# First mixer: the triangular inverse in stages of four blocks (Horner form), transposes for products, four masks for seven

## The chip, the cores and the metric

One Trainium2 chip, of which the kernel uses one core. The metric is the device time of one execution in microseconds; the time of a kernel is the median of its runs.

## The reference, cut to what matters

The program is three transformer layers in float32 over 512 tokens of width 1024. The change touches only the first mixer, a chunked gated delta rule with 8 heads of 128 columns. For each head it solves a unit lower triangular system:

```python
a_low = jnp.where(strict, jnp.einsum('bhncd,bhnsd->bhncs', k_beta, k) * decay, 0.0)
eye = jnp.eye(CHUNK, dtype=q.dtype)
rhs = jnp.concatenate([v * beta[..., None], k_beta * jnp.exp(g_cum)[..., None]], axis=-1)
sol = lax.linalg.triangular_solve(eye + a_low, rhs, left_side=True, lower=True,
                                  unit_diagonal=True)
u, w = sol[..., :dv], sol[..., dv:]
```

Around it stand the dense projection of the layer input (`proj = hn @ w_in`), a causal convolution of width 4, the norms of q and k, and the scan over chunks that uses `u` and `w`. The kernel works with chunks of 128 tokens instead of 64, so each head has four chunks (`TT = 4`) and for each a 128x128 triangle to invert.

## The kernel before, in words

Each engine has its own instruction stream, written out by hand, and the streams meet only at semaphores: the order of the lines is the order of the work.

The first mixer is a loop over eight heads, `period(p)` on every engine. On TensorE a period has 32 slots. In slot `i` stands first one dense block of the projection for head p+1 (`dense_for`: three fp32r matmuls of 128x128 by 128x512 for the high and low halves, L1716 to L1718), then what `rest_of(p-1, i)` has in that slot (the scan over chunks of the head before: w at slot 0, L1955; `vn`, L1963 and L1965; outputs and state, L1970 to L1977; the sum of squares of the output, L1981), then `front(p, i)` (rows of decays, L1894 and L1895; products of keys and queries, L1899 and L1902; transposes of k and v, L1907 and L1912; transposes of the masked matrix, L1917) and `level(p, i)`, the inverse. At slot 23 stand besides the sums of squares of the next head's q and k (`qk_sums`, L1883 and L1884). In head 0 the slots of `front` and `level` are moved by the table `FIRST_HEAD` and the sums stand at slot 24. The last head has no dense blocks of a next head; 15 blocks of the output projection stand in its even slots from 2 on (`OUT_AT`).

The inverse before goes through seven levels of blocks (1, 2, 4, ... 64). `TI` holds the inverse so far, `T` its transpose, four 128x128 matrices each. Level 0 is one minus the masked matrix (`AM`, made on GpSimd, L1615) and, through a transpose on TensorE (L1917), the same for `T`. Each of the six other levels has two steps:

- the X step (slots `X_AT`, L1930): `AM` times `T`, four fp32 matmuls of 128x128 into bank 5, which ScalarE copies to `X` (L520, `inverse_x`);
- the Y step (slots `Y_AT`): four products of `X` and `TI` into bank 6 (L1941), which VectorE subtracts from `T` (L1169), and four into bank 7 (L1944), which VectorE subtracts from `TI` (L1173). The last level has no L1941.

Four such matmuls, one for each chunk, are called a group below. The profiler records two rows of TensorE for each fp32 matmul of this kind and one for each transpose, so a group of matmuls is x8 and a group of transposes x4.

ScalarE has in a period, in this order from slot 19 on: `inverse_x(p, 3)`, the two steps of the output norm (`out_rstd`, L536 and L538), half of the split of weights (`hi_half`, L512), a load of a function table and Silu and Square of the next head's q and k (`evac_qk`, L483 and L485), and `inverse_x(p, 4)`. TensorE's `qk_sums` at slot 23 waits for the Square (semaphore `qk_sq`). Then `qk_rstds` (L491 to L494) follows. VectorE does the convolutions (L1072, L1075), the low halves of the weights (`lo_half`, L1148), the state of the scan (L1159, L1162) and the subtractions of the inverse. A dense block at slot 0 waits for VectorE's convolution of v (`conv_v`), the one at slot 16 for that of q (`conv_q`).

Of the kernel before, what the change touches and what calls it, by code (L numbers as in the profile page):

```python
# [13 lines left out]
F32 = mybir.dt.float32  # L14
F32R = mybir.dt.float32r
# [5 lines left out]
P = 128  # L21
# [11 lines left out]
LEVELS = 7  # L33
# [14 lines left out]
MATS = ("ident", "ones", "rot", "prefix", "suffix", "future", "cap", "lvl0", "lvl1", "lvl2", "lvl3", "lvl4", "lvl5", "lvl6")  # L48
# [27 lines left out]
X_AT, Y_AT = (7, 11, 15, 19, 23, 27), (9, 13, 17, 21, 25, 29)  # L76
W_AT, VN_AT, OS_AT, OSS_AT = 0, (1, 5, 9, 13), (3, 7, 11, 15), 19
FIRST_HEAD = {0: 5, 1: 6, 3: 8, 5: 10, 7: 12, 9: 13, 11: 15, 13: 16, 15: 18, 17: 20, 19: 21, 21: 23, 23: 25, 25: 26, 27: 28, 29: 30}
# [38 lines left out]
def build(nc, io):  # L117
    with ExitStack() as ctx:
# [30 lines left out]
        with ExitStack() as gdn:  # L149
# [20 lines left out]
            rows_r = sb("rows_r", [48, SEQ], F32R, gdn)  # L170
            sel = sb("sel", [48, 2, 2, P], F32R, gdn)
            ba_wh = sb("ba_wh", [P, P], F32R, gdn)
            ba_wl = sb("ba_wl", [P, P], F32R, gdn)
# [26 lines left out]
        with ExitStack() as mix:  # L200
# [24 lines left out]
            cosT, sinS = trig("prefix"), trig("lvl0")  # L225
# [61 lines left out]
        part_done = sem("part_done")  # L287
# [52 lines left out]
        def _(act):  # L340
# [103 lines left out]
            act.activation(ba_wh[:, :], ba_w, ACT.Copy)  # L444
# [108 lines left out]
            def period(p):  # L553
# [14 lines left out]
                hi_half(2 * p + 3, 0)  # L568
                if p:
                    values_out(g, 1, 2)  # L570
# [5 lines left out]
                inverse_x(p, 0)  # L576
                if p:
                    values_out(g, 2, 2)
                if last:
                    out_fill(3)  # L580
                inverse_x(p, 1)
                if p:
                    values_out(g, 3, 2)
                if last:
                    out_fill(4)
                inverse_x(p, 2)
                if p:
                    out_squares(g, 3)
                if dense:
                    hi_half(2 * p + 4, 0)  # L590
                if last:
                    out_fill(5)
                inverse_x(p, 3)
# [317 lines left out]
        def _(dve):  # L911
# [130 lines left out]
            dve.tensor_tensor(ba_wl[:, :], ba_w, ba_wh[:, :].bitcast(F32), ALU.subtract)  # L1042
# [121 lines left out]
            def inverse_y(h, n):  # L1164

                if n < 5:
                    dve.wait_ge(y_done, 11 * h + 2 * n + 1)
                    dve.wait_ge(t_made, 6 * h + n + 1)
                    dve.tensor_tensor(T[:, :, :], T[:, :, :], bank(6), ALU.subtract).then_inc(t_made, 1)  # L1169
                ti = TI[:, h % 2, :, :]  # L1170
                dve.wait_ge(y_done, 11 * h + (2 * n + 2 if n < 5 else 11))
                dve.wait_ge(ti_made, 7 * h + n + 1)
# [11 lines left out]
            def period(p):  # L1184
# [25 lines left out]
                one = mat("ident").unsqueeze(1).to_broadcast([P, TT, P])  # L1210
                dve.wait_ge(am_made, 7 * p + 1)
                dve.tensor_tensor(TI[:, r, :, :], one, AM[:, 0, :, :], ALU.subtract).then_inc(ti_made, 1)
                dve.wait_ge(amt_done, p + 1)
                dve.tensor_tensor(T[:, :, :], one, bank(4), ALU.subtract).then_inc(t_made, 1)
                if last:
                    out_low(2)
                if p:
                    state(g, 1, 2)
                lo_half(2 * p + 3, 0)
                inverse_y(p, 0)  # L1220
# [7 lines left out]
                inverse_y(p, 1)  # L1228
# [4 lines left out]
                inverse_y(p, 2)  # L1233
# [4 lines left out]
                inverse_y(p, 3)  # L1238
                if p:
                    scale_out(g, 3)  # L1240
                if dense:
                    lo_half(2 * p + 4, 0)
# [1330 lines left out]
```

## Time and profile before

| what | value |
|---|---|
| median of 3 runs | 2312.74 us (2311.11 to 2314.26) |
| profiled execution, its own time | 2316.1 us |
| its span | 2314.3 us |
| TensorE busy | 2238.7 us, 97% of the span |
| VectorE, ScalarE, GpSimd busy | 1130.4, 918.5, 323.6 us |
| TensorE's share of the chain that ended last | 90% |
| granted clock of TensorE, mean | 0.990 of 2.4 GHz |

The profiled execution is one of a kind with the others: it took 3.4 us more than the median. Busy shares are means over stages; the first mixer's eight periods lie between about 69 and 462 us of the span. In rows of the timeline, neighbouring rows of TensorE overlap, since each row holds the whole way of its columns through the array: what one group costs there is the distance from its start to the next start.

### The profile page before, as it was taken

The numbers are of one execution on the slowest core, as the hardware profiler recorded it, in microseconds if no ns is written. First come the engines' busy times: TensorE is split into PE (matmuls) and PEld (weight loads), VectorE is DVE, ScalarE is ACT, GpSimd is POOL, SyncE is SP. The second block draws the span as 40 slices with busy tenths as digits, with TensorE's granted clock in tenths as the row PEclk, the third lists the DMA queues.
The fourth block names the chain that finished last, engine by engine and source line by source line (L and its number), as shares of the span: only waits on it lengthen the run. The fifth ranks groups of instructions, "written<-read, shape, count | busy, mean of one in ns | idle before, by whom it ended". The sixth has DMA issues, their size and how long they took to land.

```text
span 2314.3 us, 28733 instructions
## 1 busy us (share of the span) xinstructions
PE 2238.7 (97%) x11172; PEld 1840.8 (80%) x11172; DVE 1130.4 (49%) x1437; ACT 918.5 (40%) x1235; POOL 323.6 (14%) x271
## 2 busy tenths in 40 slices
PE   7899999999999999998999999999999999999998
PEld 4688888778888887976788888887788787888886
DVE  4556556544444323355444442254665655655522
ACT  4444444433223225466322321244665554444311
POOL 0123222230000110001300001100100025222211
PEclk9899999999999999999999999999999999999999
DMA  3311110112222222210222222231211213222221
GB/s 135 92 55 37 41 51 37 37 73 91 101 98 91 94 106 73 92 55 19 73 96 104 91 94 106 91 133 69 69 55 69 69 37 127 97 103 91 93 108 55
DMA packets 30607, 185.61 MB, mean 80 GB/s; under 512 B 3104, under 2 KB 5536, under 8 KB 10160
## 3 DMA queue, kind: packets, MB, share of 16 engines
q1 hardware_dynamic: 28496, 176.66, 21.4%
q0 software_dynamic: 2016, 7.60, 1.0%
q8 instruction: 69, 1.13, 0.2%
q14 instruction: 26, 0.21, 0.0%
HBM read 180.02 MB, written 7.37 MB: 81 GB/s over the span
## 4 chain that ended last, share of the span: by engine, by line
PE 90%; ACT 4%; DVE 4%; issue 1%; DMA 0%; SPq 0%; POOL 0%; DVEq 0%; ACTq 0%; POOLq 0%
PE ps L1716 25%; PE ps L1718 24%; PE ps L1717 24%; PE ps L1930 1%; PE ps L1944 1%; PE ps L1941 1%; PE ps L2375 1%; PE ps L2318 1%; PE ps L2358 1%; PE ps L2155 1%; DVE convd L1075 1%; PE ps L2385 1%; PE ps L2193 1%; DVE wl L920 1%; ACT wh L349 0%
## 5 line engine op out<-in xcount | busy, mean ns | idle before, releaser
L1716 PE MATMUL ps<-xh,wh 128*128 128x512 f32 x1888 | 767.2, 406 | 30.4 <-DVE wl L920 17.1
L1718 PE MATMUL ps<-xh,wl 128*128 128x512 f32 x1888 | 740.6, 392 | 0.0
L1717 PE MATMUL ps<-xl,wh 128*128 128x512 f32 x1888 | 740.1, 392 | 0.0
L349 ACT ACTIVATE wh<-raw 128x2048 fp32r<-128x2048 f32 x144 | 275.3, 1914 | 545.0 <-PE ps L1718 544.7
L920 DVE TENSOR_TENSOR wl<-raw,wh 128x2048 fp32r<-128x2048 f32 x144 | 336.7, 2338 | 310.9 <-ACT wh L349 310.9
L1716 PEld LDWEIGHTS ps<-xh,wh 128*128 128x128 f32 x1888 | 357.8, 189 | 115.3 <-issue 26.5
L1718 PEld LDWEIGHTS ps<-xh,wl 128*128 128x128 f32 x1888 | 357.0, 189 | 76.9
L1717 PEld LDWEIGHTS ps<-xl,wh 128*128 128x128 f32 x1888 | 357.8, 190 | 71.9 <-issue 4.5
L1716 PE MATMUL ps<-hid_h,wh 128*128 128x512 f32 x528 | 208.0, 394 | 0.0
L1718 PE MATMUL ps<-hid_h,wl 128*128 128x512 f32 x528 | 207.0, 392 | 0.0
L1717 PE MATMUL ps<-hid_l,wh 128*128 128x512 f32 x528 | 204.9, 388 | 0.0
L998 DVE TENSOR_TENSOR scaled<-ps,rstd 128x1024 f32<-128x1024 f32 x44 | 53.9, 1225 | 192.9 <-PE ps L1718 192.9
L1615 POOL TENSOR_TENSOR AM<-AT,mats 128x512 f32<-128x512 f32 x56 | 76.3, 1369 | 332.2 <-DVE AT L1196 196.9
L1718 PEld LDWEIGHTS ps<-hid_h,wl 128*128 128x128 f32 x528 | 99.1, 188 | 23.2
L1717 PEld LDWEIGHTS ps<-hid_l,wh 128*128 128x128 f32 x528 | 99.1, 188 | 22.2
L1716 PEld LDWEIGHTS ps<-hid_h,wh 128*128 128x128 f32 x528 | 99.3, 188 | 19.7
L1581 POOL TENSOR_TENSOR sq<-hT 128x512 f32<-128x512 f32 x41 | 48.3, 1178 | 292.6 <-DVE hT L1032 257.6
L520 ACT ACTIVATE X<-ps 128x512 f32<-128x512 f32 x48 | 28.7, 597 | 146.9 <-PE ps L1930 146.9
L1576 POOL TENSOR_TENSOR ssq<-hT 128x512 f32<-128x512 f32 x6 | 6.2, 1041 | 563.0 <-DVE hT L1032 507.0
L1169 DVE TENSOR_TENSOR T<-T,ps 128x512 f32<-128x512 f32 x40 | 27.6, 689 | 104.6 <-PE ps L1941 104.4
L422 ACT ACTIVATE hid_h<-gu 128x512 f32 (+1 forms) x44 | 27.8, 632 | 110.2 <-DVE gu L1008 110.2
L998 DVE TENSOR_TENSOR gu<-ps,rstd 128x1024 f32<-128x1024 f32 x22 | 26.9, 1224 | 85.8 <-PE ps L1718 85.8
(343 smaller groups left out, 2938.7 us busy)
## 6 DMA issues: line engine op xcount, KB each, us to landing
raw<-in_stream SPq DMA_DIRECT2D x159, 1024.0 KB, 4.8
hankd<-tabd SPq DMA_DIRECT2D x1, 3072.0 KB, 16.9
hank<-hankd POOLq DMA_DIRECT2D x4, 768.0 KB, 5.0
hT<-in_xT SPq DMA_DIRECT2D x4, 512.0 KB, 6.0
keepd<-hT POOLq DMA_DIRECT2D x1, 2048.0 KB, 11.3
hT<-keepd POOLq DMA_DIRECT2D x8, 256.0 KB, 4.4
out<-hT SPq DMA_DIRECT2D x8, 256.0 KB, 2.1
raw<-in_stream SPq DMA_DIRECT2D x2, 512.0 KB, 9.0
```

The lines of the kernel that those rows point to most:

```text
L349: act.activation(wh[:, s, :], raw[:, s, :], ACT.Copy).then_inc(hi_made, 1)
L422: act.activation(hid_h[:, 2 * it + j, :], prod, ACT.Copy).then_inc(hid_hi_made, 1)
L520: act.activation(X[:, :, :], blocks4(5), ACT.Copy).then_inc(x_made, 1)
L920: dve.tensor_tensor(wl[:, s, :], raw[:, s, :], wh[:, s, :].bitcast(F32), ALU.subtract).then_inc(lo_made, 1)
L998: dve.tensor_tensor(to[:, :, :], ps[:, b:b + 2, :], rstd[:, :].unsqueeze(1).to_broadcast([P, 2, SEQ]), ALU.mult).then_inc(gu_made, 1)
L1075: dve.scalar_tensor_tensor(convd[:, i, d:SEQ], ps[:, b, 0:SEQ - d], w, convd[:, i, d:SEQ], ALU.mult, ALU.add).then_inc(conv_step, 1)
L1169: dve.tensor_tensor(T[:, :, :], T[:, :, :], bank(6), ALU.subtract).then_inc(t_made, 1)
L1581: pool.tensor_tensor(sq[:, :], hT[:, c, :], hT[:, c, :], ALU.mult).then_inc(squared, 1)
L1615: pool.tensor_tensor(AM[:, l % 2, :, :], AT[:, :, :], m, ALU.mult).then_inc(am_made, 1)
L1716: pe.matmul(out, w_hi, a_hi, start=start, stop=False)
L1717: pe.matmul(out, w_hi, a_lo, start=False, stop=False)
L1718: return pe.matmul(out, w_lo, a_hi, start=False, stop=stop)
```

## The change

The seven levels become four stages with blocks of 1, 4, 16 and 64 (`STAGES`), and the masks are `below1`, `below4`, `below16`, `below64`; the masks of 4 and 16 are transposed. A stage with four blocks inverts two levels at once: with M the strictly block-triangular part times the inverse of the diagonal blocks, M to the fourth power is zero and the inverse is a sum of three powers, taken in Horner form.

- Stage 0: `U` = one minus the transposed A (VectorE), then "square" and "cube" on TensorE, each `AM` times `U`, and after each one minus the product on VectorE, which gives `T`. "turn0" transposes `T` on TensorE and ScalarE copies it to `TI`.
- Stages 1 and 2: "scale" (`AM` times `TI`, a group), ScalarE's copy with sign to `X` (`inverse_x`), "first", "second", "third" (groups with `X`, after each VectorE adds `T`), and "turn" (transposes `T`), with ScalarE's copy to `TI` (`turned`).
- Last stage, two blocks: "x" and "y", as the last level before.
- A second group of transposes (of `AT`, unmasked) joins the one at slot 5, and ScalarE copies it to `DT` (`make_a`), from which GpSimd makes the two transposed masks.

The slots of the inverse, and with them those of `vn`, outputs and the sum of squares, are set anew:

```diff
-X_AT, Y_AT = (7, 11, 15, 19, 23, 27), (9, 13, 17, 21, 25, 29)
-W_AT, VN_AT, OS_AT, OSS_AT = 0, (1, 5, 9, 13), (3, 7, 11, 15), 19
+INVERSE_AT = {"square": 7, "cube": 9, "turn0": 10, "scale1": 12, "first1": 13, "second1": 15, "third1": 17, "turn1": 18,
+              "scale2": 20, "first2": 21, "second2": 23, "third2": 25, "turn2": 26, "x": 28, "y": 30}
+W_AT, VN_AT, OS_AT, OSS_AT = 0, (1, 5, 9, 15), (3, 7, 12, 17), 20
...
+            def make_a(h):
+                act.wait_ge(amt_done, h + 1)
+                act.activation(DT[:, :, :], blocks4(5), ACT.Copy).then_inc(a_made, 1)
+
+            def turned(h, n):
+                act.wait_ge(turned_done, 3 * h + n + 1)
+                act.activation(TI[:, h % 2, :, :], blocks4((4, 4, 6)[n]), ACT.Copy).then_inc(ti_made, 1)
+
             def inverse_x(h, n):
-                act.wait_ge(x_done, 6 * h + n + 1)
-                act.activation(X[:, :, :], blocks4(5), ACT.Copy).then_inc(x_made, 1)
+                act.wait_ge(x_done, 3 * h + n + 1)
+                act.activation(X[:, :, :], blocks4(5), ACT.Copy, scale=1.0 if n == 2 else -1.0).then_inc(x_made, 1)
...
                 hi_half(2 * p + 3, 0)
+                make_a(p)
                 if p:
                     values_out(g, 1, 2)
                 hi_half(2 * p + 3, 1)
...
-                inverse_x(p, 3)
+                inverse_x(p, 1)
                 if p:
                     out_rstd(g, 2)
                 if dense:
                     hi_half(2 * p + 4, 1)
                     evac_qk(p + 1)
-                inverse_x(p, 4)
-                if dense:
                     qk_rstds(p + 1)
-                inverse_x(p, 5)
+                turned(p, 2)
+                inverse_x(p, 2)
...
+            def inverse_t(h, n):
+
+                bank_of = (4, 6, 7, 6, 7, 6, 7, 6, 7)
+                dve.wait_ge(*((amt_done, h + 1) if n == 0 else (y_done, 9 * h + n)))
+                if n:
+                    dve.wait_ge(t_made, 9 * h + n)
+                if n < 3:
+                    one = mat("ident").unsqueeze(1).to_broadcast([P, TT, P])
+                    dve.tensor_tensor((T if n == 2 else U)[:, :, :], one, bank(bank_of[n]), ALU.subtract).then_inc(t_made, 1)
+                else:
+                    dve.tensor_tensor((T if n % 3 == 2 else U)[:, :, :], T[:, :, :], bank(bank_of[n]), ALU.add).then_inc(t_made, 1)
...
                 elif slot == AMT_AT:
-                    pe.wait_ge(am_made, 7 * p + 1)
+                    pe.wait_ge(am_made, 4 * p + 1)
+                    pe.wait_ge(attn_made, p + 1)
                     for c in range(TT):
                         m = pe.transpose(ps[:, 4, cs(c)], AM[:, 0, c, :], mat("ident"))
+                    for c in range(TT):
+                        m = pe.transpose(ps[:, 5, cs(c)], AT[:, c, :], mat("ident"))
                     m.then_inc(amt_done, 1)
...
+                    elif name[:4] == "turn":
+                        pe.wait_ge(t_made, 9 * p + 3 * k + 3)
                         for c in range(TT):
+                            m = pe.transpose(ps[:, (4, 4, 6)[k], cs(c)], T[:, c, :], mat("ident"))
+                        m.then_inc(turned_done, 1)
+                    elif name[:5] == "scale":
+                        pe.wait_ge(ti_made, 4 * p + k)
+                        pe.wait_ge(am_made, 4 * p + k + 1)
+                        if k == 1:
+                            pe.wait_ge(a_made, p + 1)
+                        each(5, AM[:, k % 2, :, :], ti).then_inc(x_done, 1)
+                    elif name[:5] == "first":
+                        pe.wait_ge(x_made, 3 * p + k)
+                        each(5 + k, X, T).then_inc(y_done, 1)
+                    elif name[:6] == "second":
+                        pe.wait_ge(t_made, 9 * p + 3 * k + 1)
+                        each(8 - k, X, U).then_inc(y_done, 1)
+                    elif name[:5] == "third":
+                        pe.wait_ge(t_made, 9 * p + 3 * k + 2)
+                        each(5 + k, X, U).then_inc(y_done, 1)
```

How the order changes on TensorE, in a middle head, from the sum of squares of the output (L1981) to the sums for q and k (L1883, L1884). Before, with slots 19 to 23; the groups x4 are the inverse:

```order
L1981 MATMUL ps<-on,mats 128x512
L1930 MATMUL ps<-T,AM 128x128 x4
L1716 MATMUL ps<-xh,wh 128x512
L1717 MATMUL ps<-xl,wh 128x512
L1718 MATMUL ps<-xh,wl 128x512
...
L1941 MATMUL ps<-X,TI 128x128 x4
L1944 MATMUL ps<-TI,X 128x128 x4
...
L1930 MATMUL ps<-T,AM 128x128 x4
L1883 MATMUL ps<-sqk,mats 128x512
L1884 MATMUL ps<-sqk,mats 128x512
```

The first "..." is one more dense block (slot 21), the second is two (slots 22 and 23). Of the change, slots 20 to 23, where "..." is the two dense blocks of slots 22 and 23 (L1941 is here "scale2", "first2" and "second2" in turn, L2021 the sum of squares, L1900 and L1901 the sums for q and k):

```order
L2021 MATMUL ps<-on,mats 128x512
L1941 MATMUL ps<-TI,AM 128x128 x4
L1733 MATMUL ps<-xh,wh 128x512
L1734 MATMUL ps<-xl,wh 128x512
L1735 MATMUL ps<-xh,wl 128x512
L1941 MATMUL ps<-T,X 128x128 x4
...
L1941 MATMUL ps<-U,X 128x128 x4
L1900 MATMUL ps<-sqk,mats 128x512
L1901 MATMUL ps<-sqk,mats 128x512
```

Between the group that ScalarE's `inverse_x` waits for and the sums stood four dense blocks and three groups; now three dense blocks and two groups stand there.

On ScalarE, the same place before (from L520, `inverse_x(p, 3)`, to the reciprocal roots of q and k, L494, and the last `inverse_x`):

```order
L520 ACTIVATE X<-ps 128x512
L536 ACTIVATE on<-ps,vec 128x512
L538 ACTIVATE on<-on 128x512
L512 ACTIVATE wh<-raw 128x1024
L483 ACT_TABLE_LOAD
L483 ACTIVATE qkvz<-convd 128x1024
L485 ACTIVATE sqk<-qkvz 128x1024
L520 ACTIVATE X<-ps 128x512
L353 ACT_TABLE_LOAD
L491 ACTIVATE sqk<-ps,vec 128x512
L492 ACTIVATE sqk<-ps,vec 128x512
L494 ACTIVATE sqk<-sqk 128x1024
```

And of the change (L530 is `inverse_x`, L526 `turned`):

```order
L530 ACTIVATE X<-ps 128x512
L546 ACTIVATE on<-ps,vec 128x512
L548 ACTIVATE on<-on 128x512
L514 ACTIVATE wh<-raw 128x1024
L485 ACT_TABLE_LOAD
L485 ACTIVATE qkvz<-convd 128x1024
L487 ACTIVATE sqk<-qkvz 128x1024
L355 ACT_TABLE_LOAD
L493 ACTIVATE sqk<-ps,vec 128x512
L494 ACTIVATE sqk<-ps,vec 128x512
L496 ACTIVATE sqk<-sqk 128x1024
L526 ACTIVATE TI<-ps 128x512
```

From the copy of `X` to the Square nothing is moved; the copy of `X` behind the Square is gone and `turned` stands behind the roots.

On TensorE, slots 9 to 12 of the change, where "cube" and "turn0" (L1962) follow each other with one dense block between, and "scale1" comes after the outputs of the scan:

```order
L1941 MATMUL ps<-U,AM 128x128 x4
L1733 MATMUL ps<-xh,wh 128x512
L1734 MATMUL ps<-xl,wh 128x512
L1735 MATMUL ps<-xh,wl 128x512
L1962 MATMUL ps<-mats,T 128x128 x4
...
L2010 MATMUL ps<-qd,S 128x128
L2015 MATMUL ps<-attnT,vn 128x128
L2017 MATMUL ps<-vn,kd 128x128
L1941 MATMUL ps<-TI,AM 128x128 x4
```

Before, in a middle head, every two neighbouring groups of the inverse that wait for each other had two dense blocks between them; now "cube" and "turn0", "scale1" and "first1", "third1" and "turn1", "scale2" and "first2", "third2" and "turn2" have one.

## Rows read from the trace of the kernel before

**Rows 1.** The page: busy time and instructions of each engine

```profile
PE 2238.7 (97%) x11172; PEld 1840.8 (80%) x11172; DVE 1130.4 (49%) x1437; ACT 918.5 (40%) x1235; POOL 323.6 (14%) x271
```

**Rows 2.** Windows, heads 1 to 6: busy us by engine, granted clock, DMA

```profile
118.49:419.29 300.80, 293.76 (x1859) 254.44 (x1857) 178.93 (x270) 138.29 (x199) 77.02 (x54) 1.00 0.12 42
```

**Rows 3.** Timeline of TensorE, head 3: start, us, instruction, idle before it

```profile
225.09 0.60 PE L1907 MATMUL ps<-mats,qkvz 128*128 128x128 f32 x4
225.53 0.60 PE L1912 MATMUL ps<-mats,qkvz 128*128 128x128 f32 x4
...
227.79 0.60 PE L1917 MATMUL ps<-mats,AM 128*128 128x128 f32 x4
...
249.50 1.05 PE L1930 MATMUL ps<-T,AM 128*128 128x128 f32 x8
...
251.78 1.05 PE L1941 MATMUL ps<-X,TI 128*128 128x128 f32 x8
252.67 1.06 PE L1944 MATMUL ps<-TI,X 128*128 128x128 f32 x8
253.49 0.47 PE L1716 MATMUL ps<-xh,wh 128*128 128x512 f32 x1
...
254.26 0.40 PE L1716 MATMUL ps<-xh,wh 128*128 128x512 f32 x1
...
254.95 1.05 PE L1930 MATMUL ps<-T,AM 128*128 128x128 f32 x8
256.89 1.12 PE L1883 MATMUL ps<-sqk,mats 128*128 128x512 f32 x2 [0.88 <-ACT sqk L485]
```

**Rows 4.** Timeline of VectorE, head 3

```profile
228.43 0.69 DVE L1214 TENSOR_TENSOR T<-mats,ps 128x512 f32<-128x512 f32 x1 [0.16 <-PE ps L1917]
...
252.87 0.69 DVE L1169 TENSOR_TENSOR T<-T,ps 128x512 f32<-128x512 f32 x1 [1.73 <-PE ps L1941]
```

**Rows 5.** Timeline of ScalarE, head 3

```profile
250.59 0.60 ACT L520 ACTIVATE X<-ps 128x512 f32<-128x512 f32 x1 [4.15 <-PE ps L1930]
...
255.78 1.06 ACT L485 ACTIVATE sqk<-qkvz 128x1024 f32<-128x1024 f32 x1
```

**Rows 6.** Timeline of TensorE, the start of head 4

```profile
268.17 0.50 PE L1716 MATMUL ps<-xh,wh 128*128 128x512 f32 x1 [0.19 <-DVE convd L1075]
...
268.98 1.05 PE L1955 MATMUL ps<-TI,kbe 128*128 128x128 f32 x8
```

**Rows 7.** Timeline of TensorE, last head

```profile
419.29 1.16 PE L1955 MATMUL ps<-TI,kbe 128*128 128x128 f32 x8 [0.78 <-DVE TI L1173]
...
457.81 1.05 PE L1930 MATMUL ps<-T,AM 128*128 128x128 f32 x8
...
459.55 1.16 PE L1944 MATMUL ps<-TI,X 128*128 128x128 f32 x8
...
461.48 1.16 PE L1955 MATMUL ps<-TI,kbe 128*128 128x128 f32 x8
```

**Rows 8.** Timeline of TensorE, head 0 and the start of head 1

```profile
87.78 0.50 PE L1716 MATMUL ps<-xh,wh 128*128 128x512 f32 x1 [2.65 <-DVE convd L1075]
...
88.58 1.70 PE L1941 MATMUL ps<-X,TI 128*128 128x128 f32 x8
...
91.64 0.74 PE L1716 MATMUL ps<-xh,wh 128*128 128x512 f32 x1
...
104.28 1.13 PE L1883 MATMUL ps<-sqk,mats 128*128 128x512 f32 x2 [1.24 <-ACT sqk L485]
...
117.69 0.50 PE L1716 MATMUL ps<-xh,wh 128*128 128x512 f32 x1 [1.84 <-DVE convd L1075]
...
118.49 1.05 PE L1955 MATMUL ps<-TI,kbe 128*128 128x128 f32 x8
```

**Rows 9.** Windows behind two idle times of TensorE: columns as in rows 2

```profile
88.60:91.90 3.30, 3.30 (x18) 3.30 (x17) 0.69 (x1) 0.00 (x0) 0.00 (x0) 0.53 0.13 52
119.30:122.60 3.30, 3.30 (x24) 2.69 (x23) 1.67 (x5) 1.99 (x4) 0.00 (x0) 1.00 0.00 0
```

More of the change, by code:

```diff
@@ L32 @@
 NEG = -1e30
-LEVELS = 7
+STAGES = (1, 4, 16, 64)
 LN_EXP_SET = 6
@@ L1209, in period @@
                     out_low(1)
[L1210 to L1214, printed above, removed]
+                inverse_t(p, 0)
                 if last:
@@ L1602, in period @@
                 g, r = p - 1, p % 2
-                for l in range(LEVELS):
-                    if l == 0:
+                for n, size in enumerate(STAGES):
+                    if n == 0:
                         pool.wait_ge(at_made, p + 1)
-                    elif l == 2:
+                    elif n == 1:
                         pool.wait_ge(eg_made, p + 1)
@@ L1914, in front, with each @@
                 elif slot == AMT_AT:
-                    pe.wait_ge(am_made, 7 * p + 1)
+                    pe.wait_ge(am_made, 4 * p + 1)
+                    pe.wait_ge(attn_made, p + 1)
                     for c in range(TT):
                         m = pe.transpose(ps[:, 4, cs(c)], AM[:, 0, c, :], mat("ident"))
+                    for c in range(TT):
+                        m = pe.transpose(ps[:, 5, cs(c)], AT[:, c, :], mat("ident"))
                     m.then_inc(amt_done, 1)
+            def each(b, left, right):
+                for c in range(TT):
+                    m = pe.matmul(ps[:, b, cs(c)], left[:, c, :], right[:, c, :], start=True, stop=True)
+                return m
@@ L1937, in level @@
                         pe.wait_ge(kdkbe_made, p + 1)
+                        each(6, AM[:, 0, :, :], U).then_inc(y_done, 1)
+                    elif name == "cube":
+                        pe.wait_ge(t_made, 9 * p + 2)
                         pe.wait_ge(vb_made, p + 1)
[L1939 removed]
+                        each(7, AM[:, 0, :, :], U).then_inc(y_done, 1)
+                    elif name[:4] == "turn":
+                        pe.wait_ge(t_made, 9 * p + 3 * k + 3)
                         for c in range(TT):
[L1941 to L1942 removed]
@@ L1943, in level @@
-                    for c in range(TT):
-                        m = pe.matmul(ps[:, 7, cs(c)], X[:, c, :], ti[:, c, :], start=True, stop=True)
-                    m.then_inc(y_done, 1)
+                            m = pe.transpose(ps[:, (4, 4, 6)[k], cs(c)], T[:, c, :], mat("ident"))
[15 more added lines that the diff above has]
+                        each(5 + k, X, U).then_inc(y_done, 1)
+                    elif name == "x":
+                        pe.wait_ge(ti_made, 4 * p + 3)
+                        pe.wait_ge(am_made, 4 * p + 4)
+                        each(5, AM[:, 1, :, :], T).then_inc(x_done, 1)
+                    else:
+                        pe.wait_ge(x_made, 3 * p + 3)
+                        each(7, X, ti).then_inc(y_done, 1)
```

106 lines of the change are left out of this document (47 added, 59 removed).

## The prediction

> **What bounds the kernel now.** I read the page first: TensorE is busy for 2238.7 us [rows 1]. In heads 1 to 6 of the first mixer it is busy for 293.76 of 300.80 us [rows 2], so a head takes 300.80 / 6 = 50.13 us and hardly more than its TensorE work. Next I read the timeline of one middle head, TensorE first, and looked at every idle time with its releaser. There are two in a head. One is 0.88 us ahead of the sums for q and k, released by ScalarE's Square [rows 3]; the other is 0.19 us at slot 0, released by the convolution of v [rows 6]. Measured from the time at which TensorE could have gone on, they cost more: the X group starts at 254.95 and takes 0.89, so the sums could have started at 255.84 and did at 256.89, 1.05 us later. At slot 0 the like comes to about 0.45 us. So in a middle head 50.13 = 48.6 of work + 1.5 of waiting. Then the two ends: head 0, which waits longer (2.65, 1.24, 1.84 us) [rows 8], and the last head, which has few dense blocks to cover its chain.
>
> **Prices.** From start to next start a group of four fp32 matmuls takes 252.67 - 251.78 = 0.89 us. A group of four transposes takes 225.53 - 225.09 = 0.44. Of two dense blocks behind a group the first takes 0.77 and the second 0.69 [rows 3]; the group ahead of them then counts 0.82, so I take 0.89 and 0.70 throughout and nothing for the switch. From the start of a group to the engine that reads its bank: 252.87 - 251.78 = 1.09 us; 0.64 for transposes [rows 3, 4]. ScalarE then takes 0.60, VectorE 0.69 [rows 4, 5], and TensorE goes on about 0.05 later (Square's end 256.84, sums 256.89 [rows 3, 5]). A chain group, block, group takes 1.59 us without a wait. Through ScalarE it took 459.55 - 457.81 = 1.74 [rows 7], and the group behind such a wait takes some 0.10 more. I price a link through ScalarE with one block as cover at 0.25 us, one through VectorE, 0.09 slower, at 0.35.
>
> **What goes and comes on TensorE.** A head had 17 groups of matmuls and one of transposes in its inverse. Now it has 12 and 5: square, cube, two times (scale, first, second, third), x, y; and two at slot 5, three turns. That is 5 x 0.89 - 4 x 0.44 = 2.69 us less work in a head, 21.5 us in eight, if nothing waits. Work in a middle head falls from 48.6 to 45.9.
>
> A rule speaks to the size of this. The Trainium skill, page "TensorE: Matmul & The Clock Gate", section "Terms", calls the transpose mode four times faster for FP32. By that a group of transposes would be 0.22 us and a head would save 5 x 0.89 - 4 x 0.22 = 3.57, so 0.9 more; eight heads would give 2308 instead of my 2315.5 if none of it were lost to waits. The rows show half the price of a matmul group, not a quarter, and I stay with them.
>
> **What waits instead, middle head.** Five links now have one block as cover. Cube to turn0, third1 to turn1 and third2 to turn2 go through VectorE: 3 x 0.35. Scale1 to first1 and scale2 to first2 go through ScalarE: 2 x 0.25. Together 1.55 us. The others have two blocks, or a block and work of the scan, and I find them covered: square to cube has 1.4 of blocks and 0.44 of `vn` against 0.69 of VectorE; second1 to third1 the same. VectorE's 1.22 us of `lo_half` lies between square and cube and ends 0.8 us before cube does. GpSimd's masks are each asked for 4 us or more after their input is there. The convolution of q ends 0.3 us before slot 16 asks for it, that of v 0.2 us before slot 0; a delay there would cost itself. The 0.45 at slot 0 goes.
>
> The large one is ahead of the sums. ScalarE goes from the copy of `X` through `out_rstd`, `hi_half`, a table load, Silu and Square without a stop: 250.59 to 256.84, 6.25 us [rows 5], and this series is not changed. So the sums start 1.09 + 6.25 + 0.05 = 7.39 us after the start of the group that this copy waits for. Before, that group was X at slot 19 (249.50), and TensorE had 6.34 us of work until the sums. Now it is scale2 at slot 20, with scale2 itself, three blocks, first2 with its wait of 0.25, and second2 behind it: 3 x 0.89 + 3 x 0.70 + 0.25 = 5.0. The wait is 7.39 - 5.0 = 2.4 us in place of 1.05. In idle time as the timeline counts it, about 2.25.
>
> Sum for a middle head: 45.9 + 1.55 + 2.4 = 49.85 against 50.13, so -0.3 us, and -1.8 for six. A second way gives -0.45: scale2 starts 0.2 us later in its head than X did (one block more, two groups and a bit less), and behind the sums there are two groups and a wait less in work: -0.65 + 0.2. I keep the first.
>
> **Head 0.** I walked it by the same prices. Before, the convolution of q, which VectorE starts only after two subtractions, held slot 16 to 87.78 [rows 8]. Now it comes at 87.4, but three groups that stood ahead of the sums for q and k no longer do: TensorE has scale2 at 95.9, ScalarE's series (without `out_rstd`, 5.1 us from the copy's start) ends at 102.5, and the sums start there instead of at 104.28. The wait ahead of them is 2.7 us idle instead of 1.24. Behind them TensorE needs 12.6 us until head 1, which starts at 115.1 instead of 118.49: -3.4 us. The walk has an error of 1 to 1.5 us.
>
> **The last head.** It has 15 blocks as cover and no sums. Its chain is longer now: 12 links of 1.8 and three turns of 1.3 against 12 of 1.8. ScalarE's `make_a`, ahead of `values_out` and the fill of the third chunk, delays VectorE's `out_low` and with it square to cube by some 1.2 us, first1 and first2 have no block in their slots (0.85 each), and y now stands in the last slot but one with nothing behind it. Walked from the transposes at slot 5, the last w group starts at 462.7 against 461.48 [rows 7]: +1.2 us.
>
> **The clock.** In head 0 idle time of 2.65 us was followed by a granted clock of 0.53, which is 1.2 GHz, while 1.84 us was followed by 1.00 [rows 8, 9]. Two groups that take 1.71 then took 91.64 - 88.58 = 3.06, and the block behind them 0.25 more: 1.6 us for one fall. The new waits lie between these rows: 2.25 in six heads, 2.7 in head 0. Nothing in the trace of before says whether 2.25 does it. Bounds are none of the seven and all seven; I count head 0's and 3.5 of the other six, 4.5 falls. Part of a fall may lie in the wait itself, so 1.5 us each: +6.8. The fall that head 0 had before, behind 2.65 us, is on the side of before in the 3.4; its wait of now (2.2 idle) could fall as well, which is in the range.
>
> **Sum.** -1.8 - 3.4 + 1.2 = -4.0 without the clock, +2.8 with it. The profiled execution took 2316.1, so 2318.9 for its like; it lies 3.4 us above the median, and the difference is what carries over: 2312.7 + 2.8 = 2315.5.
>
> **Rivals.** Within 0.2% is within 4.6 us, about what a measurement of this kernel can tell from no change.
>
> (a) The forecast: the wait ahead of the sums grows, the clock falls behind some of the seven. 2311 to 2319. Chance 0.45.
>
> (b) The wait grows, and the clock falls behind none or one: 2312.7 - 4.0 = 2308.7, up to 2310. For it: the clock held at 1.84 us. Against: it fell at 2.65. Chance 0.2.
>
> (c) The clock falls in every head, twice in head 0: eight falls are +12, 2312.7 - 4.0 + 12 = 2320.7; this is the slower side. It decides from 2.25 us of idle time being enough. For it: six heads are alike, so what one does the others may do. Against: the wait need not lie the same way each time, and the fall adds to the head's length. Chance 0.22. The Trainium skill, same page, section "Part 4: PE-mode transpose", says that a transpose does not count as busy TensorE for the clock; with 28 transposes in a head where 12 were, that speaks for this case. The transposes at slot 3 in the old trace ran at full clock, but nothing there puts them beside a long wait.
>
> (d) The sums don't wait longer, because ScalarE gets through earlier than I read, and only the five short links cost: 45.9 + 1.55 = 47.45 in a head, -2.7 x 6 - 3.4 + 1.2 = -18.4, 2294. Against it stands that this series on ScalarE is the same instruction for instruction. Chance 0.07.
>
> (e) A delay on VectorE in each head: the convolution of q or v comes late, with margins of 0.2 to 0.3 us. A GpSimd mask beside `lo_half` could add 0.75. On top of the forecast that is +4, 2319. Chance 0.06.
>
> **How the numbers follow.** Likeliest is (a), 2315.5. The range from 2306 to 2322 takes in (a), (b), (c) and (e) with an error of 2 us of the walks, and leaves out (d) and the far ends. Faster by over 0.2% (under 2308.1): (d) and half of (b), 0.18. Slower (over 2317.3): (c), half of (e), and the upper part of (a), 0.32. The rest is 0.50.
>
> **What would show it.** In the new trace: 12 groups of inverse matmuls and 5 of its transposes in a head instead of 17 and 1; the sums for q and k wait for Square with about 2.2 us in heads 1 to 6; short waits of 0.1 to 0.3 for VectorE at the turns; w groups 49.8 us apart where the clock holds and 51.3 where it falls; granted clock 0.5 behind some of the waits; about 43.4 us from the last head's first w group to the next. It is wrong if the wait ahead of the sums is under 1.5 us, or if a releaser that I called covered (convolution, mask, `lo_half`) heads the list of waits.

## The result and the profile after

The changed kernel takes 2316.18 us (median of 22 runs, 2314.18 to 2319.83) against 2312.68 (22 runs, 2310.82 to 2315.56): a ratio of 1.0015, interval 1.0008 to 1.0021. It is 3.5 us slower, a difference that the interval tells from zero, and lies within 0.2% of before. Its profiled execution took 2318.6 us with a span of 2316.5, at a mean granted clock of 0.987 against 0.990 before.

The first rows of the page, busy time of each engine:

```profile
PE 2231.8 (96%) x10980; PEld 1817.9 (78%) x10980; DVE 1117.2 (48%) x1413; ACT 924.4 (40%) x1243; POOL 283.5 (12%) x247
```

TensorE is busy for 6.9 us less than before [rows 1], GpSimd for 40, and still the kernel is not faster. The timeline of TensorE in a middle head, from the scale group of stage 2 to the first w group, columns: start, duration, engine, line, operation, operands, shapes and count, and in brackets idle time and its releaser:

```profile
191.45 0.66 PE L1962 MATMUL ps<-mats,T 128*128 128x128 f32 x4
...
194.19 1.05 PE L1941 MATMUL ps<-TI,AM 128*128 128x128 f32 x8
...
195.94 1.16 PE L1941 MATMUL ps<-T,X 128*128 128x128 f32 x8
...
198.32 1.05 PE L1941 MATMUL ps<-U,X 128*128 128x128 f32 x8
201.59 1.12 PE L1900 MATMUL ps<-sqk,mats 128*128 128x512 f32 x2 [2.21 <-ACT sqk L487]
202.55 1.85 PE L1901 MATMUL ps<-sqk,mats 128*128 128x512 f32 x2
203.41 1.42 PE L1733 MATMUL ps<-xh,wh 128*128 128x512 f32 x1
204.62 0.63 PE L1734 MATMUL ps<-xl,wh 128*128 128x512 f32 x1
205.05 0.63 PE L1735 MATMUL ps<-xh,wl 128*128 128x512 f32 x1
...
206.42 1.05 PE L1941 MATMUL ps<-U,X 128*128 128x128 f32 x8
...
208.26 0.66 PE L1962 MATMUL ps<-mats,T 128*128 128x128 f32 x4
```

L1941 is now every group of the inverse, L1962 a turn, L1900 and L1901 the sums for q and k, L1733 to L1735 a dense block. The sums wait 2.21 us for Square where it was 0.88 [rows 3]. From the start of scale2 to the sums it is 201.59 - 194.19 = 7.40 us, and ScalarE's series in that time:

```profile
195.28 0.60 ACT L530 ACTIVATE X<-ps 128x512 f32<-128x512 f32 x1 [2.54 <-PE ps L1941]
195.78 0.68 ACT L546 ACTIVATE on<-ps,vec 128x512 f32<-128x512 f32 x1
196.49 0.63 ACT L548 ACTIVATE on<-on 128x512 f32<-128x512 f32 x1
197.03 1.05 ACT L514 ACTIVATE wh<-raw 128x1024 fp32r<-128x1024 f32 x1
198.09 1.28 ACT L485 ACT_TABLE_LOAD   x1
199.39 1.06 ACT L485 ACTIVATE qkvz<-convd 128x1024 f32<-128x1024 f32 x1
200.48 1.06 ACT L487 ACTIVATE sqk<-qkvz 128x1024 f32<-128x1024 f32 x1
```

It has no gap, and takes 201.54 - 195.28 = 6.26 us, as it did [rows 5]. In the TensorE rows behind the sums a dense row lasts 0.63 where it otherwise lasts 0.39 to 0.40: the clock. The view by windows, columns us, then TensorE, its weight loads, VectorE, ScalarE and GpSimd, then granted clock, DMA share and GB/s; first the wait and the sums, then what follows; next two stretches of head 1, whose sums start at 151.82 behind a wait of the same length; last the stretch behind the start of the sums of head 6, at 407.22:

```profile
199.19:202.60 3.41, 1.20 (x5) 0.54 (x4) 1.49 (x3) 3.35 (x4) 1.27 (x1) 1.00 0.00 0
202.70:206.00 3.30, 3.30 (x8) 1.89 (x7) 0.00 (x0) 1.67 (x4) 0.00 (x0) 0.50 0.00 0
151.50:154.80 3.30, 2.98 (x10) 1.81 (x10) 0.00 (x0) 2.51 (x4) 0.83 (x1) 1.00 0.00 0
154.90:158.20 3.30, 3.22 (x21) 2.56 (x20) 2.08 (x4) 1.86 (x3) 0.00 (x0) 1.00 0.00 0
407.50:410.80 3.30, 3.30 (x5) 1.22 (x5) 0.00 (x0) 0.97 (x1) 0.23 (x1) 0.50 0.00 0
```

In this head the clock falls to 0.50, 1.2 GHz, about 1 us after TensorE goes on, and stays there for about 3.4 us. About half of that is lost: by the lengths of the heads below, 1.6 us. In the heads that follow the fall begins earlier, and in head 6 it takes in nearly all of the sums. And the stretches from one first w group to the next, of TensorE alone: head 1, head 2, head 6 and the last.

```profile
113.55:163.30 49.75, 47.29 (x288) 1.00 0.13 45
163.30:214.69 51.39, 48.94 (x287) 0.97 0.11 42
368.94:419.94 51.00, 48.46 (x285) 0.97 0.11 39
419.94:463.20 43.26, 37.37 (x231) 0.96 0.09 31
```

A head whose clock holds takes 49.75 us against 50.13; one in which it falls 51.39 to 51.43 (heads 3 to 5 are as head 2). Head 1 alone held, heads 2 to 6 fell. In head 0 it fell twice:

```profile
82.68 0.50 PE L1733 MATMUL ps<-xh,wh 128*128 128x512 f32 x1 [2.22 <-DVE convd L1084]
...
99.46 1.38 PE L1900 MATMUL ps<-sqk,mats 128*128 128x512 f32 x2 [2.54 <-ACT sqk L487]
```

**Where the mixer's time went in these two traces.** From the rows of decays of head 0 to its first w group it is 48.54 us against 48.69 (65.01 to 113.55, and 69.80 to 118.49): -0.15. Heads 1 to 6 take 306.39 us against 300.80 [rows 2]: +5.6. The last head takes 43.26 against 42.19 [rows 7]: +1.07. Together +6.5. The profiled executions differ by 2.5 us only, since the one of before comes to head 0 4.8 us later (69.80 against 65.01), though both programs do the same work on TensorE up to there. Most of that, 3.6 us, comes about between 11 and 28 us, with a granted clock of 0.57 from 20 to 24 us where the one of after had 1.00 (windows of TensorE alone, before and then after):

```profile
20.00:24.00 4.00, 2.52 (x7) 0.57 0.00 0
20.00:24.00 4.00, 3.89 (x18) 1.00 0.13 20
```

Such falls outside the mixer come and go from one execution to the next: in the nine traces of the changed kernel and its variants below, which are the same program up to there, head 0 starts between 64.53 and 68.61 us. So the medians, 3.5 apart, are the measure of the change, and one trace against another is read by stretches only.

### The profile page after: what moved, and what is told of

The parts are those of the page before. It is cut to its first block, busy times and chain, and to the rows that moved or that the text cites. A ratio compares the mean times of both kernels' runs of the same rounds, so it can differ in the third digit from the quotient of the medians.

```text
span 2316.5 us, 28229 instructions
## 1 busy us (share of the span) xinstructions
PE 2231.8 (96%) x10980; PEld 1817.9 (78%) x10980; DVE 1117.2 (48%) x1413; ACT 924.4 (40%) x1243; POOL 283.5 (12%) x247
## 4 chain that ended last, share of the span: by engine, by line
PE 91%; ACT 4%; DVE 4%; issue 1%; DMA 0%; POOL 0%; SPq 0%; DVEq 0%; ACTq 0%; POOLq 0%
PE ps L1733 25%; PE ps L1735 24%; PE ps L1734 24%; PE ps L1941 3%; PE ps L2415 1%; PE ps L2358 1%; PE ps L2398 1%; PE ps L2195 1%; PE ps L2425 1%; PE ps L2233 1%; PE ps L1962 1%; DVE wl L929 1%; PE ps L1901 1%; PE ps L1900 0%; DVE T L1183 0%
## 5 line engine op out<-in xcount | busy, mean ns | idle before, releaser
L1733 PE MATMUL ps<-xh,wh 128*128 128x512 f32 x1888 | 772.1, 409 | 25.8 <-DVE wl L929 17.1
L1735 PE MATMUL ps<-xh,wl 128*128 128x512 f32 x1888 | 741.1, 393 | 0.0
L1733 PEld LDWEIGHTS ps<-xh,wh 128*128 128x128 f32 x1888 | 358.8, 190 | 109.0 <-issue 26.0
L1735 PEld LDWEIGHTS ps<-xh,wl 128*128 128x128 f32 x1888 | 357.4, 189 | 76.8
L1733 PE MATMUL ps<-hid_h,wh 128*128 128x512 f32 x528 | 208.0, 394 | 0.0
L1735 PE MATMUL ps<-hid_h,wl 128*128 128x512 f32 x528 | 207.0, 392 | 0.0
L1735 PEld LDWEIGHTS ps<-hid_h,wl 128*128 128x128 f32 x528 | 99.1, 188 | 23.2
L1733 PEld LDWEIGHTS ps<-hid_h,wh 128*128 128x128 f32 x528 | 99.3, 188 | 19.7
L1599 POOL TENSOR_TENSOR ssq<-ssq,sq 128x512 f32<-128x512 f32 x41 | 61.4, 1497 | 3.2
L827 ACT ACTIVATE prob<-ps,nmax 128x512 f32<-128x512 f32 x32 | 22.0, 689 | 89.4 <-DVE nmax L1484 89.2
L1084 DVE SCALAR_TENSOR_TENSOR convd<-ps,vec,convd 128x511 f32<-128x511 f32 (+2 forms) x72 | 53.8, 748 | 2.3
```

Of the source, the lines that this page charges most:

```text
L1084: dve.scalar_tensor_tensor(convd[:, i, d:SEQ], ps[:, b, 0:SEQ - d], w, convd[:, i, d:SEQ], ALU.mult, ALU.add).then_inc(conv_step, 1)
L1599: pool.tensor_tensor(ssq[:, :], ssq[:, :], sq[:, :], ALU.add).then_inc(summed, 1)
L1733: pe.matmul(out, w_hi, a_hi, start=start, stop=False)
L1735: return pe.matmul(out, w_lo, a_hi, start=False, stop=stop)
```

## The experiments

Kernels are compared with runs of the kernel before on the same chip: medians 2313.49 us for the first four, 2313.83 for the next four and 2313.01 for the last two. "A head" is the distance between first w groups of two middle heads in the trace.

**Theory.** The Horner form itself gains about 5 us, and the falls of the clock behind the longer wait ahead of the sums take more than that. Rivals: the length of the wait costs, not the clock; or transposes let the clock fall.

### Filling the wait: matmuls, transposes

Work that nobody reads goes into the idle time, so that TensorE is busy while the sums still start when Square is done. It adds work and takes none away. With matmuls:

```diff
+                if n:
+                    for _ in range(9):
+                        pe.matmul(ps[:, 4, :], wh[:, 1, 0:P], xh[:, 0, :], start=True, stop=True)
                 pe.wait_ge(qk_sq, n + 1)
```

> The changed kernel with nine extra fp32r matmuls (0.23 us each, 2.1 us in all, into bank 4, which the sums overwrite) ahead of the wait for Square in each of the seven heads that have the sums. They fit into the wait of 2.2 us idle, so nothing else moves. Theory (the falls of the clock behind this wait cost 1.6 us each): no granted clock of 0.5 behind the sums in any head, the middle heads all 49.75 us apart, and 5 to 6 falls fewer: 8 to 10 us less than the changed kernel, about 2307. Rival (the longer wait and the longer chain are the loss, and the clock is a symptom that other waits hide): within 1 us of the changed kernel, 2316.

And with transposes in their place:

```diff
+                if n:
+                    for k in range(20):
+                        pe.transpose(ps[:, 4, (k % 4) * P:(k % 4 + 1) * P], T[:, k % 4, :], mat("ident"))
                 pe.wait_ge(qk_sq, n + 1)
```

> As fill_mm, with twenty transposes of 128x128 (0.11 us each, 2.2 us in all) in place of the nine matmuls. If transposes keep the clock up as matmuls do: the same 2307. If a transpose does not count as busy TensorE for the clock: falls as in the changed kernel, 2316.

Matmuls: 2307.96 us (11 runs, 2305.92 to 2310.0), ratio 0.9978 (0.9969 to 0.9987). Transposes: 2306.76 us (11 runs, 2304.7 to 2309.82), ratio 0.9971 (0.9962 to 0.998). The timeline of TensorE in a middle head with the matmuls, and the window behind the sums:

```profile
198.05 2.30 PE L1899 MATMUL ps<-xh,wh 128*128 128x512 f32 x9
200.51 1.12 PE L1903 MATMUL ps<-sqk,mats 128*128 128x512 f32 x2 [0.16 <-ACT sqk L487]
201.47 1.02 PE L1904 MATMUL ps<-sqk,mats 128*128 128x512 f32 x2
201.93 0.79 PE L1733 MATMUL ps<-xh,wh 128*128 128x512 f32 x1
202.56 0.40 PE L1734 MATMUL ps<-xl,wh 128*128 128x512 f32 x1
```

```profile
200.60:203.90 3.30, 3.30 (x12) 2.10 (x13) 0.00 (x0) 2.50 (x4) 0.44 (x1) 1.00 0.00 0
```

The same two views with the transposes:

```profile
200.80 2.35 PE L1899 MATMUL ps<-mats,T 128*128 128x128 f32 x20
203.17 1.13 PE L1903 MATMUL ps<-sqk,mats 128*128 128x512 f32 x2
```

```profile
203.20:206.50 3.30, 3.30 (x12) 2.07 (x13) 0.00 (x0) 2.50 (x4) 0.50 (x1) 1.00 0.00 0
```

The sums start no earlier in their head (a head is 49.75 us in both), and in no head does the clock fall behind them. In head 0 the fall behind the wait for the convolution of q is still there in both (from about 84.9 us with the matmuls). In the last head the clock holds in both, at 1.00 as a mean of the head with the matmuls, behind a wait of 3.18 us that is still there; after the change and before it, it falls there. So the wait costs what it is long, and the falls come on top: 2316.18 - 2307.96 = 8.2 us by the medians. Without them the changed kernel is 5.5 us faster than before, of which 1.6 may be the fall in the last head, that the kernel before has as well. Transposes do as well as matmuls: the two medians differ by 1.2 us and their ranges overlap. The Trainium skill, page "TensorE: Matmul & The Clock Gate", section "Part 4: PE-mode transpose", says that a transpose does not count as TensorE activity for the clock in the way that a matmul does. These rows disagree for transposes in fp32: twenty of them, 2.35 us, did what nine matmuls, 2.30 us, did.

### The sums two slots later

```diff
-ROWS_AT, KK_AT, KT_AT, AMT_AT, SUMS_AT = 0, 1, 3, 5, 23
+ROWS_AT, KK_AT, KT_AT, AMT_AT, SUMS_AT = 0, 1, 3, 5, 25
...
-                    if i == (SUMS_AT if p else 24) and p < HEADS - 1:
+                    if i == (SUMS_AT if p else 26) and p < HEADS - 1:
```

> The changed kernel with the sums for q and k two slots later: slot 25 instead of 23, and 26 instead of 24 in head 0. ScalarE's Square is not moved, so the sums start at the same time; two blocks and the group third2 now stand ahead of them. Theory (the wait ahead of the sums is the loss): that wait falls to 0.2 us, no clock falls behind it; but the chain from Square over the roots, scale_qk, lo_half and the convolution of v to slot 0 is not shorter and becomes the bound, so a middle head is about 49.1 us, and x waits some 0.8 us for ScalarE. 13 us less in heads 1 to 6 and 2 to 3 in head 0: 2300. Rival (turns and one-block links are the loss): two waits of 0.3 less at most, 2312 or more.

And in the kernel before, one slot later:

```diff
-ROWS_AT, KK_AT, KT_AT, AMT_AT, SUMS_AT = 0, 1, 3, 5, 23
+ROWS_AT, KK_AT, KT_AT, AMT_AT, SUMS_AT = 0, 1, 3, 5, 24
...
-                    if i == (SUMS_AT if p else 24) and p < HEADS - 1:
+                    if i == (SUMS_AT if p else 25) and p < HEADS - 1:
```

> The kernel before with its sums one slot later (24, and 25 in head 0). Control: what the kernel before has to gain from its own wait ahead of the sums, 1.05 us a head. The chain from Square to the convolution of v to slot 0 stays, and it already held slot 0 by 0.45 us, so it takes back the 0.7 us of the block that now stands ahead: 2312 to 2313, no change. If that chain is not what bounds it: 0.7 x 7 less, 2308.

The changed kernel: 2305.18 us (5 runs, 2301.31 to 2307.2), ratio 0.9962 (0.9948 to 0.9976). The kernel before: 2305.89 us (5 runs, 2303.08 to 2306.12), ratio 0.9965 (0.9951 to 0.9978). In the first a head is 49.0 us, as expected, and the clock holds in heads 1 to 6. But two other waits came up in it. The timeline of TensorE:

```profile
200.61 1.12 PE L1900 MATMUL ps<-sqk,mats 128*128 128x512 f32 x2
...
205.52 1.16 PE L1941 MATMUL ps<-T,AM 128*128 128x128 f32 x8 [0.39 <-ACT TI L526]
...
210.51 0.51 PE L1733 MATMUL ps<-xh,wh 128*128 128x512 f32 x1 [0.86 <-DVE convd L1084]
```

The 2300 us expected was missed by 5. In the trace heads 1 to 6 are 7.0 us shorter than before (113.31 to 407.08 against 300.80), head 0 is 3.2 shorter (67.78 to 113.31 against 48.69) and the last head 1.05 longer, together -9.1; in head 0 a part of what was gained at the sums came back as a wait of 1.29 us for the convolution of v. The miss is not in these heads. Against the trace of the changed kernel heads 1 to 6 are 12.6 us shorter (293.77 against 306.39) and head 0 is 3.0 shorter (45.53 against 48.54), as expected. But I took the 16 us from the median of the changed kernel, 2316.2, while the gain was read from its trace, 2318.6, which by the sum near the end of this document has more falls than the median; and this execution came to head 0 at 67.78 in place of 65.01. In the kernel before, a head went from 50.15 to 49.48 us, and its slot 0 waits as long as it did:

```profile
199.14 1.13 PE L1883 MATMUL ps<-sqk,mats 128*128 128x512 f32 x2 [0.19 <-ACT sqk L485]
...
209.73 0.50 PE L1716 MATMUL ps<-xh,wh 128*128 128x512 f32 x1 [0.19 <-DVE convd L1075]
```

There my expectation of no change was wrong. I had thought that the chain from Square to the convolution of v bound that kernel. It doesn't: that convolution stands on VectorE behind a subtraction that one of TensorE's own groups releases, and the roots of q and k are ready before that subtraction ends (before, in head 2, at 211.1 us against 212.6), so it moves forward with TensorE. The plain lesson is that 7.6 us lay in the sums' slot before the change as well, so the moved slot is no merit of the Horner form.

### The next wait: the convolution of v

On VectorE `conv_v(p + 1)` stood behind half a split of weights (`lo_half`) near the end of the period. Moved ahead, on top of the later sums:

```diff
                     scale_out(g, 3)
+                if dense:
+                    conv_v(p + 1)
                 inverse_t(p, 8)
...
                     lo_half(2 * p + 4, 1)
-                    conv_v(p + 1)
                 inverse_last(p)
```

> sums25 with the convolution of v (four instructions of VectorE, 3.1 us) moved up, from behind lo_half to behind scale_out, where VectorE idles for 5 to 7 us. In sums25 a middle head takes 49.0 us with 0.86 us idle (about 1.0) at slot 0 for this convolution. Theory: that wait goes and nothing takes its place; 48.0 us a head, 7 us less than sums25 in all, 2298. Rival (slot 0 then waits for lo_half or w waits for the last subtraction by as much): 2304 to 2305, with another releaser at slot 0.

The same move alone, with the sums left at slot 23:

> The changed kernel with its sums where they are and only the convolution of v moved up. Control: the convolution does not bind the changed kernel, because the wait ahead of the sums covers it. Theory: no change against the changed kernel, 2316, with the clock falling behind the sums as there. Rival (the convolution is what costs the changed kernel its gain): 2310 or less.

On top of the later sums: 2293.04 us (4 runs, 2290.52 to 2297.88), ratio 0.9907 (0.9891 to 0.9922), a head 47.87 us. That is 12 us less than with the later sums alone, where I had expected 7: in the traces heads 1 to 6 are 7.0 us shorter, as expected (286.74 against 293.77), head 0 is 1.6 shorter (68.26 to 112.15), and the last head is 1.6 shorter (41.63 against 43.24), since the clock did not fall in it this time. Alone: 2319.78 us (10 runs, 2315.77 to 2321.84), ratio 1.0026 (1.0017 to 1.0036). So the move is worth 12 us behind one repair and nothing, or a loss, without it. Alone it leaves the wait ahead of the sums at 2.21 us with the falls in heads 0 and 3 to 6 of its trace, heads without a fall at 49.75, and adds a wait in head 0, where the convolution now delays VectorE's subtraction ahead of turn2:

```profile
108.57 0.66 PE L1963 MATMUL ps<-mats,T 128*128 128x128 f32 x4 [1.75 <-DVE T L1183]
```

I had expected 2316 there. Head 0 is 1.5 us longer than in the changed kernel (64.53 to 114.58 against 48.54). For the rest of the 3.6 us between the medians the mean clock speaks: six of the ten runs had 0.985 or 0.986, of the changed kernel's 22 runs four, so its usual execution seems to have more falls than the one in the trace. That was not seen directly. Against the kernel before, each on its own chip, the two differ by 2.5 us (+5.95 and +3.5).

### The wait for TI at the last stage

The group x reads `T` and `AM`, not `TI`; its wait for the turned `TI` can stand ahead of y. On top of the last kernel:

```diff
                     elif name == "x":
-                        pe.wait_ge(ti_made, 4 * p + 3)
                         pe.wait_ge(am_made, 4 * p + 4)
...
                         pe.wait_ge(x_made, 3 * p + 3)
+                        pe.wait_ge(ti_made, 4 * p + 3)
                         each(7, X, ti).then_inc(y_done, 1)
```

> convv with the wait for turned (TI) moved from x, which does not read TI, to y. In sums25 x waits 0.4 us idle (about 0.5). Theory: 47.5 us a head, 3 us less than convv, 2295. Rival (the wait only moves to y): as convv.

2292.33 us (4 runs, 2289.91 to 2293.14), ratio 0.9905 (0.989 to 0.992). A head is 47.56 us, 0.31 less than with the wait at x, in agreement with its place; the difference of the medians, 0.7 us, is too small to count by itself. A head of the trace has hardly any wait left. The window of one head, TensorE alone:

```profile
111.65:159.19 47.54, 47.23 (x287) 1.00 0.13 48
```

### The kernel before with the same two repairs

The later sums, and `conv_v` ahead of the split of weights:

```diff
                     lo_half(2 * p + 4, 0)
+                    conv_v(p + 1)
                 inverse_y(p, 4)
...
                     lo_half(2 * p + 4, 1)
-                    conv_v(p + 1)
                 inverse_y(p, 5)
```

> The kernel before with its sums a slot later and the convolution of v moved up ahead of the fifth Y step, the same two repairs as in convv. Its head has 48.6 us of work and 49.48 in before_sums24, with 0.45 us at slot 0. Theory: 48.9 to 49.0 a head, 4 us less than before_sums24, about 2302. So with both kernels repaired the Horner form is ahead by about 1.4 us a head, some 7 us (best1 against this). Rival (the Horner form has no lead once its own short links are paid): best1 within 2 us of this.

2299.82 us (5 runs, 2298.87 to 2301.0), ratio 0.9941 (0.9927 to 0.9954), a head 49.02 us. Against 2292.33 the Horner form is ahead by 7.5 us, and in a head by 49.02 - 47.56 = 1.46 us. This is what the change is worth once its neighbours let it: about half of the 2.69 us of work that it saves in a head. The two kernels are not repaired quite alike. The changed one has its sums two slots later and this one a single slot, and the wait for `TI` moved ahead of y has no counterpart here. Without that move, 2293.04 and 47.87, the lead is 6.8 us, and 1.15 us in a head.

### Head 0's wait for the convolution of q

On top of the best kernel, in head 0 half of `conv_q(1)` a subtraction earlier, and that kernel again beside it:

```diff
                 inverse_t(p, 0)
+                if p == 0:
+                    conv_q(1, (0, 1))
...
-                    conv_q(p + 1, (0, 1) if p else range(4))
+                    conv_q(p + 1, (0, 1) if p else (2, 3))
```

> best1 with, in head 0 only, the first two of the four instructions of the convolution of q moved up to behind the first subtraction of the inverse, where VectorE idles. In best1 slot 16 of head 0 waits 2.22 us idle for this convolution, and the clock falls behind it. Theory: the wait falls to 0.7 us and no clock falls there: 1.5 + 1.6 = 3.1 us less than best1, 2289. Rival (the convolution delays square to cube, and head 0 loses at slot 13 what it gains at slot 16): within 1 us of best1 but still no fall.

> best1 once more, on the chip of best2, so that the two are compared under the same conditions: 2292, and middle heads 47.56 us apart.

2292.3 us (5 runs, 2288.54 to 2292.58) and 2292.66 us (5 runs, 2291.84 to 2295.66), ratios 0.9911 (0.9898 to 0.9925) and 0.9915 (0.9901 to 0.9928). The wait at slot 16, first with the earlier half and then without, timelines of TensorE:

```profile
81.29 0.50 PE L1736 MATMUL ps<-xh,wh 128*128 128x512 f32 x1 [0.65 <-DVE convd L1084]
81.62 0.40 PE L1737 MATMUL ps<-xl,wh 128*128 128x512 f32 x1
```

```profile
84.81 0.50 PE L1734 MATMUL ps<-xh,wh 128*128 128x512 f32 x1 [2.22 <-DVE convd L1084]
...
86.19 0.63 PE L1736 MATMUL ps<-xh,wl 128*128 128x512 f32 x1
86.62 1.91 PE L1942 MATMUL ps<-T,X 128*128 128x128 f32 x8
```

The wait shrinks by 1.57 us and the fall behind it goes; in the traces head 0 is shorter by 2.8 us (65.22 to 105.90 against 67.18 to 110.69). But the medians differ by 0.4 us with intervals that overlap, so the 2289 us that I expected did not come: only the profiled execution, 2288.54, is there, and the other four took 2291.65 to 2292.58. Whether the 2.8 us hold over many runs is open.

## Why the prediction was right

The forecast of 2315.5 us lies 0.7 from 2316.18, and the way there held step by step.

- **Prices.** From cube to turn0 it took 231.16 - 229.33 = 1.83 us, a link of 0.24 over 1.59, where I had 0.35 for VectorE; third1 to turn1 and third2 to turn2 came to 0.25 each. Scale2 to first2 took 1.75, and first2 then 0.10 more than a group behind a block: 0.26, where I had 0.25 for ScalarE. Rows of cube and turn0:

```profile
229.33 1.06 PE L1941 MATMUL ps<-U,AM 128*128 128x128 f32 x8
...
231.16 0.66 PE L1962 MATMUL ps<-mats,T 128*128 128x128 f32 x4
```

  The five links together were about 1.26 us, not 1.55. The busy time agrees with the prices: before 48.96 us in a head [rows 2], less 2.69, plus 1.01 of the links, is 47.28, and the row above has 47.29. The 1.01 is what of the links does not count as idle time, since the rows ahead of them still last: idle in a head is 49.75 - 47.29 = 2.46, of which 2.21 is the wait ahead of the sums, and 1.26 - 0.25 = 1.01. A group of transposes still costs 0.41 to 0.44, half of a group of matmuls.
- **The wait ahead of the sums.** 7.40 us from scale2 to the sums against 7.39, and 2.21 us of idle time in heads 1 to 6 against 2.25. The step that TensorE's shorter work only lengthens its wait for an unchanged series on ScalarE is what the trace shows, and the fills and the later sums confirm it.
- **A middle head.** 49.75 us without a fall against 49.85, 51.4 with one against 51.3 to 51.4.
- **Head 0.** -0.15 us with two falls. At 1.6 each they are 3.2, so -3.35 without them; the walk gave -3.4, with the waits 2.54 and 2.22 where it had 2.7 and 2.2. That head 0's second wait might fall too was named in the range and not in the sum.
- **The last head.** 463.20 - 419.94 = 43.26 against 42.19, +1.07; forecast +1.2. Its terms agree less well than its sum. Scale1 to first1 took 1.75 us (440.72 to 442.47), 0.86 more than a group, as priced. But square to cube took 2.50 us (434.43 to 436.93), where a middle head less one block gives 2.73 - 0.69 = 2.04: `make_a` and what hangs on it cost at most 0.5, not 1.2.
- **The clock.** Bounded, not known. The profiled execution has seven falls, two in head 0 and five in heads 2 to 6, nearly rival (c)'s eight (and one in the last head, as before). Seven of 1.6 are 11.2 us. By the medians it is less: +3.5 with -4.9 for the rest (next point) leaves 8.4 us, about five falls; this takes it that the two kernels lose the same outside the mixer at their medians, which no run shows. I had 4.5 of 1.5, 6.8 us: 1.6 too low. I had let a part of a fall lie in the wait itself, but in the trace every fall begins after TensorE has gone on, so each costs its whole 1.6.
- **The sum.** Without the falls I had -4.0. The traces show -2.65 for heads 1 to 6 (five times -0.4, and -0.65 for the sixth, 49.31 us with the matmuls in the wait against 419.29 - 369.33 = 49.96), -3.35 for head 0 and +1.07 for the last: -4.9. The two misses, 0.9 and 1.6, point opposite ways, and that only 0.7 us is left of them is luck in part.

The rivals: (b) is what the kernel does when the falls are taken away, 2308.0 with the matmuls against its 2308.7. (c) is close to one execution but not to the median. (d) is out, the wait is there. (e) is out here: no convolution waits in the middle heads of the changed kernel. Its margins were real, though, and it is what came up, at 0.86 us a head, as soon as the sums stood later.

What stays open is why one execution has more falls than another. The recorded mean clock goes with the time: of the 22 runs the four at 0.988 average 2314.6 us, fourteen at 0.987 2316.4, three at 0.986 2317.4, and the one at 0.985 took 2319.8. That points to a number of falls that varies, but not to where: the falls ahead of the mixer vary too, and only one execution of this kernel was seen in a trace.

## What to carry to other kernels

When work is taken off the engine that bounds a kernel, look first at what it waits for at a fixed place: here a ScalarE series of 6.3 us of unchanged length turned 2.69 us of saved work in a head into 1.3 us more of waiting and a fall of the clock. Move the waiting instruction behind work that does not need it (two slots here, -11 us), then read the trace again, since the next wait (the convolution of v, -12 us) is not seen until the first is gone, and its repair alone gives nothing. Judge the idea by giving the old kernel the same repairs: 2299.8 against 2292.3 says what the Horner form is worth, and 2312.7 against 2316.2 does not.

## What the runs showed of the hardware

- A wait of the same length was followed by a fall in one head and not in another. Behind the 2.21 us of head 1 the granted clock stayed at 1.00, behind the 2.21 us of heads 2 to 6, in the same program and with the same work around it, it fell to 0.50. Behind the waits of head 0 of 2.22 to 2.23, 2.54 to 2.55 and 2.65 to 2.66 us it fell in every trace in which they stand. Behind 3.18 us in the last head it fell before and after the change, and held in both filled kernels and in the one with the later sums and the convolution moved. Behind 1.84, 1.75 and less it held in all eight heads of every trace. So length alone doesn't decide. The head in which it held:

```profile
151.82 1.13 PE L1900 MATMUL ps<-sqk,mats 128*128 128x512 f32 x2 [2.21 <-ACT sqk L487]
152.78 1.02 PE L1901 MATMUL ps<-sqk,mats 128*128 128x512 f32 x2
153.24 0.79 PE L1733 MATMUL ps<-xh,wh 128*128 128x512 f32 x1
```

- Once the clock fell behind the sums of a middle head it fell behind those of every middle head that followed, and heads 2 to 5 are alike to 0.04 us (51.39 to 51.43). In the kernel with only the convolution moved it held in heads 1 and 2 and fell from head 3 on. Against the waits the falls move forward from head to head: the first row of the sums lasts 1.12 us in head 2 and 1.29, 1.50, 1.70 and 1.93 in heads 3 to 6, each with the same 2.21 us of idle time ahead of it. What sets their place was not tested. The last of them:

```profile
407.22 1.93 PE L1900 MATMUL ps<-sqk,mats 128*128 128x512 f32 x2 [2.21 <-ACT sqk L487]
```

- A fall is late and short. Behind the sums it begins 1.0 us after TensorE has gone back to work in head 2 and 0.1 us after in head 6, in head 0 of the kernel with the matmuls 1.3 us after the wait for the convolution of q. It lasts 3.4 us at 1.2 GHz and costs 1.6 us. It is not seen at the wait itself but in longer rows behind it: 0.63 in place of 0.39 for a dense row.
- Falls that have nothing to do with the change come and go between executions: ahead of the mixer the granted clock from 20 to 24 us was 0.57 in the trace of before and 1.00 in that of after.
- Twenty fp32 transposes, 2.35 us, kept the clock up as well as nine matmuls of 2.30 us did.
